# Sums of squares placed half a block later, and the norm of a gated mixing applied behind its matmul

## The reference

```python
def rms_norm(x, g):
    y = x * rsqrt(mean(x * x, axis=-1) + 1e-6)
    return y * g

def swiglu_ffn(h, w_in, w_out):
    gate, up = split(h @ w_in, 2)
    return (silu(gate) * up) @ w_out

def gmlp_chunk_mix(h, w_uv, v_norm, w_s, b_s, w_o):
    u, v = split(gelu(h @ w_uv), 2)          # 2048 features each
    v = rms_norm(v, v_norm)
    sv = einsum('gts,bcsgd->bctgd', tril(w_s), v) + b_s   # mixes the tokens of a chunk of 128
    return (u * sv) @ w_o

for i in range(2):
    x = x + 0.5 * swiglu_ffn(rms_norm(x, ...), ...)
    h = rms_norm(x, mix_norm[i])
    x = x + (rwkv7_time_mix(h) if i == 0 else gmlp_chunk_mix(h))
    x = x + cross_attention(rms_norm(x, ...), memory)
    x = x + 0.5 * swiglu_ffn(rms_norm(x, ...), ...)
```

## Time and profile before

| what | value |
|---|---|
| median of 3 runs | 2070.46 us (2066.52 to 2074.31) |
| the profiled execution | 2068.08 us |
| its span | 2065.9 us |
| granted TensorE clock, mean | 0.98 |
| TensorE busy | 1936.4 us, 94% |
| VectorE busy | 1332.2 us, 64% |
| ScalarE busy | 1054.7 us, 51% |
| weights moved | 288 transfers of 1024 KB |

### The profile page before, as it was taken

One profiled execution on the slowest core, in us unless ns is written; L12 is line 12 of the kernel. 1 busy time (PEld: TensorE's weight loads), 2 busy tenths in 40 slices (PEclk: granted clock), 3 DMA queues, 4 the chain that ended last, 5 costly groups with the idle time before them and its releaser, 6 DMA issues.

```text
span 2065.9 us, 43633 instructions
## 1 busy us (share of the span) xinstructions
PE 1936.4 (94%) x18364; PEld 1892.0 (92%) x18364; DVE 1332.2 (64%) x1652; ACT 1054.7 (51%) x1373; POOL 57.8 (3%) x44
## 2 busy tenths in 40 slices
PE   5999998999998999998988999999999798999998
PEld 5998997899998999997887999999999797999998
DVE  6586579677776755798444665557555646556555
ACT  6555565855556444576523554445444455545443
POOL 0020000000000000000060000000000000000000
PEclk9999999999999999999999999999999899999999
DMA  5743332254553555443400435444455352434553
GB/s 197 227 157 137 135 131 103 102 184 165 185 187 134 183 181 182 145 164 123 144 4 6 161 116 182 181 181 174 175 181 181 133 182 105 166 122 176 181 183 110
DMA packets 51881, 313.35 MB, mean 152 GB/s; under 512 B 13489, under 2 KB 13617, under 8 KB 14257
## 3 DMA queue, kind: packets, MB, share of 16 engines
q1 hardware_dynamic: 51328, 308.42, 42.0%
q10 hardware_dynamic: 432, 3.15, 0.4%
HBM read 310.50 MB, written 1.05 MB: 151 GB/s over the span
## 4 chain that ended last, share of the span: by engine, by line
PE 70%; DVE 18%; ACT 6%; issue 4%; DMA 1%; DVEq 0%; ACTq 0%; SPq 0%
PE ps L282 62%; DVE wl L1892 5%; ACT wh L1267 2%; PE ps L766 2%; DVE pages L2334 1%; DVE work L1921 1%; DMA raw<-in_stream 1%; DVE pages L2149 1%; DVE pages L2396 1%; DVE pages L2151 1%; DVE pages_r L1909 1%; PE ps L941 1%; DVE pages L1965 1%; PE ps L752 1%; DVE h_r L1950 1%
## 5 line engine op out<-in xcount | busy, mean ns | idle before, releaser
L1892 DVE TENSOR_TENSOR wl<-raw,wh 128x1024 fp32r<-128x1024 f32 x576 | 701.3, 1233 | 532.5 <-ACT wh L1267 530.7
L1267 ACT ACTIVATE wh<-raw 128x1024 fp32r<-128x1024 f32 x576 | 597.6, 1052 | 456.2 <-PE ps L282 402.2
L282 PE MATMUL ps<-sq_r,wh 128*128 128x256 f32 x2592 | 742.7, 287 | 15.9 <-DVE h_r L1909 8.3
L282 PE MATMUL ps<-sq_r,wl 128*128 128x256 f32 x2592 | 735.7, 284 | 0.0
L282 PE MATMUL ps<-h_r,wh 128*128 128x256 f32 x2560 | 726.8, 284 | 0.0
L282 PE MATMUL ps<-pages_r,wh 128*128 128x256 f32 x2480 | 548.5, 287 | 33.8 <-DVE pages_r L1909 14.2
L282 PEld LDWEIGHTS ps<-sq_r,wh 128*128 128x128 f32 x2592 | 500.1, 193 | 20.8 <-issue 16.7
L282 PEld LDWEIGHTS ps<-sq_r,wl 128*128 128x128 f32 x2592 | 500.0, 193 | 0.0
L282 PEld LDWEIGHTS ps<-h_r,wh 128*128 128x128 f32 x2560 | 494.1, 193 | 0.5
L282 PE MATMUL ps<-pages_r,wl 128*128 128x256 f32 x1680 | 479.4, 285 | 0.0
L282 PEld LDWEIGHTS ps<-pages_r,wh 128*128 128x128 f32 x2480 | 425.9, 195 | 38.1 <-issue 26.8
(11 more groups left out here) (309 smaller groups left out, 1813.6 us busy)
## 6 DMA issues: line engine op xcount, KB each, us to landing
raw<-in_stream SPq DMA_DIRECT2D x288, 1024.0 KB, 4.8
pages<-in_rpb SPq DMA_DIRECT2D x32, 64.0 KB, 6.5
pages<-in_mem SPq DMA_DIRECT2D x1, 1024.0 KB, 4.9
x<-in_x SPq DMA_DIRECT2D x1, 1024.0 KB, 12.6
pages<-in_mem ACTq DMA_DIRECT2D x1, 1024.0 KB, 4.9
pages<-in_gmlp_b ACTq DMA_DIRECT2D x1, 1024.0 KB, 4.7
pages<-in_gmlp_w ACTq DMA_DIRECT2D x1, 1024.0 KB, 6.8
out<-h SPq DMA_DIRECT2D x4, 256.0 KB, 2.4
```

What stands on the lines that cost most here:

```text
L282: mm = pe.matmul(out, left, right, start=start and q == 0, stop=stop and q == 2, skip_group_check=True)
L1267: f(t.wh[(2 * b0 + hf) % PIECE_SLOTS][:], t.raw[b0 % 2][:, hf * 1024:(hf + 1) * 1024], ACT.Copy).then_inc(s["high_done"], 1)
L1892: tt(t.wl[i][:], t.raw[b0 % 2][:, hf * 1024:(hf + 1) * 1024], t.wh[i][:].bitcast(F32), ALU.subtract).then_inc(s["low_done"], 1)
```

## The change

It has three parts.

1. At `ffn0` to `ffn4`, TensorE's sums of squares move from between the first and the second weight block to the middle of the second one, behind its first half (the new `between` of `up_block`). ScalarE's `high(b + 1)` moves ahead of the first gate step.
2. At `x0` and `x1` the sum moves behind the whole second block, and `high`/`low` of block 1 move ahead of `norm_root` and of the wait for `norm_std`.
3. `mix2` becomes a late norm. `gm_u` is read out by VectorE, scaled by `rstd` (`gate_half`), and ScalarE applies GELU in place. For `gm_v`, whose product is token-major, TensorE makes the sum of squares also as one number per partition (four matmuls with one column into bank 5), ScalarE takes Ln and Exp of it into `stat`, and uses it as the scale of the GELU, which takes two activations of 256 columns instead of one of 512. The two loops over `gm_u` become straight code.

```diff
-LATE = ("ffn0", "ffn1", "x0", "ffn2", "ffn3", "x1", "ffn4")
+LATE = ("ffn0", "ffn1", "x0", "ffn2", "ffn3", "mix2", "x1", "ffn4")
...
-    def up_block(n, bank, b, act, name=None):
+    def up_block(n, bank, b, act, name=None, between=lambda: None):
         for hf in range(2):
+            if hf:
+                between()
             up_piece(n, bank, b, hf, act, name)
...
         up_block(n, n % BANKS, b, norm_parts, name)
-        if f == 1:
-            norm_sum("mem2")
-        norm_sum(name)
-        if f == 1:
-            first_norm_sum(name)
-        up_block(n + 1, (n + 1) % BANKS, b + 1, norm_parts)
+
+        def sums():
+            if f == 1:
+                norm_sum("mem2")
+            norm_sum(name)
+            if f == 1:
+                first_norm_sum(name)
+
+        up_block(n + 1, (n + 1) % BANKS, b + 1, norm_parts, between=sums)
...
         project(f"xq{i}", norm_parts, n=1, name=name)
+        project(f"xq{i}", norm_parts, first=1, n=1)
         norm_sum(name)
-        project(f"xq{i}", norm_parts, first=1, n=2)
+        project(f"xq{i}", norm_parts, first=2, n=1)
...
+    project("gm_u", norm_parts, n=2, name="mix2")
+    pe.wait_ge(s["norm_part"], 2 * NORM["mix2"] + 2)
+    for hf in range(2):
+        for b in range(TB):
+            at_ = hf * T + b * P
+            pe.matmul(ps[:, 5, b:b + 1], norm_partial(t, "mix2")[:, at_:at_ + P], cst(t, "ones")[:, 0:1],
+                      start=hf == 0 and b == 0, stop=hf == 1, skip_group_check=True)
     norm_sum("mix2")
-    operand("mix2")
-    project("gm_u", norm_parts, groups=2)
+    project("gm_u", norm_parts, first=2, n=2)
+    project("gm_u", norm_parts, first=4)
     project("gm_v", norm_parts, groups=2, token=True)
...
+        high(b + 1)
         early(0, 0, 0, True)
-        high(b + 1)
         late(0, 0, 0, True)
...
         late_norm(f"x{i}", prev)
-        highs(f"xq{i}", n=1)
+        highs(f"xq{i}", n=2)
         norm_root(f"x{i}")
-        highs(f"xq{i}", 1, 2)
+        highs(f"xq{i}", 2, 1)
...
-    norm("mix2", last_down(3))
-    take_groups("gm_u", 0, 0, 2, ACT.Gelu_apprx_tanh)
-    v2 = t.pages[:, 2 * FP:4 * FP].rearrange("p (b c) -> p b c", b=TB)
+    late_norm("mix2", last_down(3))
+    highs("gm_u", n=2)
+    act.wait_ge(s["norm_sum"], NORM["mix2"] + 1)
+    f(t.stat[:, 44:46], ps[:, 5, 0:TB], ACT.Ln, scale=1.0 / D, bias=t.stat[:, COL_EPS:COL_EPS + 1]).then_inc(s["gm_root"], 1)
+    norm_root("mix2")
+    act.wait_ge(s["gm_root"], 1)
+    f(t.stat[:, 44:46], t.stat[:, 44:46], ACT.Exp, scale=-0.5).then_inc(s["gm_root"], 1)
+    for k in range(1, 9):
+        if 1 < k < 8:
+            high(BLK["gm_u"] + k)
+        c = slice((k - 1) * 512, k * 512)
+        act.wait_ge(s["u_evac"], SEG["gm_u"] + k)
+        f(t.pages[:, c], t.pages[:, c], ACT.Gelu_apprx_tanh).then_inc(s["gm_up"], 1)
+    act.wait_ge(s["gm_root"], 2)
     for k in range(8):
         high(BLK["gm_v"] + k)
         n, c = SEG["gm_v"] + k, slice(k * 256, (k + 1) * 256)
-        take(n, n % BANKS, BLK["gm_v"] + k, v2[:, :, c], ACT.Gelu_apprx_tanh)
+        act.wait_ge(s["piece_done"], 2 * (BLK["gm_v"] + k) + 2)
+        for b in range(TB):
+            ins = f(t.page[2 + b][:, c], ps[:, n % BANKS, b * 256:(b + 1) * 256], ACT.Gelu_apprx_tanh,
+                    scale=t.stat[:, 44 + b:45 + b])
+        ins.then_inc(s["u_evac"], 1)
...
-        lows(f"xq{i}", n=1)
+        lows(f"xq{i}", n=2)
...
-            if k:
+            if k > 1:
                 low(BLK[f"xq{i}"] + k)
...
-    swiglu(3, "ffn3", last_down(2))
-
-
-    norm("mix2", last_down(3))
+    swiglu(3, "ffn3", last_down(2), "mix2")
+    late_norm("mix2", last_down(3))
+    lows("gm_u", n=2)
+    dve.wait_ge(s["norm_std"], NORM["mix2"] + 1)
+
+    def gate_half(k):
+
+        dve.wait_ge(s["piece_done"], 2 * (BLK["gm_u"] + k) + 2)
+        scaled(t.pages[:, k * 512:(k + 1) * 512],
+               ps[:, (SEG["gm_u"] + k) % BANKS, :].rearrange("p (n t) -> p n t", n=2), 2).then_inc(s["u_evac"], 1)
+
+    gate_half(0)
+    gate_half(1)
+    lows("gm_u", 2, 1)
     dve.wait_ge(s["rows_in"], 32)
...
-    low_groups("gm_u", 0, 2)
+    for k in range(2, 8):
+        gate_half(k)
+        if k < 7:
+            lows("gm_u", k + 1, 1)
     low_groups("gm_v", 0, 2)
+    dve.wait_ge(s["gm_up"], 8)
     dve.wait_ge(s["gm_vnorm"], 8)
```

More of the change, by code:

```diff
@@ L126 @@
 rw_ds0 rw_ds1 rw_s0 rw_s1 rw_turn rw_yt rw_sq rw_var rw_varsb
-rw_std rw_out fin_gain fin_log fin_inv fin_log2 fin_logs fin_std gm_vnorm gm_vstd gm_vout0 gm_vout1 gm_mask gm_mix gm_mixed
+rw_std rw_out fin_gain fin_log fin_inv fin_log2 fin_logs fin_std gm_vnorm gm_vstd gm_vout0 gm_vout1 gm_mask gm_mix gm_mixed gm_root gm_up
 """.split()
```

## The result

The changed kernel takes 2044.15 us (median of 4 runs, 2041.44 to 2047.07), the kernel before 2069.26 us in the same comparison (2066.52 to 2074.31). The ratio is 0.9873, with a 95% interval of 0.9851 to 0.9895: the change makes the kernel 1.3% faster. The prediction was 2048.5 us with a range of 2042 to 2057.

The account below looks back on a forecast made before the run. The kernel was taken as a chain of matmuls on TensorE, busy 94%. 12.7 + 9.6 - 0.3 = 22.0 us off the profiled 2068.1 gave 2046.1; with 2.4 us for the median, 2048.5 us, range 2042 to 2057.

Parts of the forecast that it names:

- The stop at `mix2`: Before `gm_u`, TensorE's 14.11 us stop and 1.77 us of slow matmuls go; net 12.7 us won after added costs.
- the 0.3 of the tail: At the last `gm_v` block, two activations instead of one delay the token mixing: 0.3 us lost.
- the lower bound: Eight one-column passes at `mix2`: at least 0.12 us each, 0.96 us together; 1.0 us taken, 1.7 us from above.
- The moved sums: At ffn0 to ffn4, x0 and x1, TensorE's waits before the sums of squares vanish: 9.6 us won.
- the same 0.1 for each on top: At each of seven moved sums, 0.1 us is added to the 8.9 us of named waits, giving 9.6 us.
- four passes need 0.86: At `ffn3`, the sum's four passes take 0.86 us of the 2.65 us seen, so 1.79 us is saved.
- The slack in the feed-forwards: ScalarE's SiLU slips 2 us behind `high(b + 1)`; an estimated 5 us remain before the first down projection, least at `ffn1`.
- The slack at the attentions: At x0 and x1 the scaled query is ready 5.3 us after block 1, wanted at 6.6 us: 1.3 us slack.
- The slack at `ffn1`: Before the first down projection of `ffn1`, TensorE arrives 0.9 us sooner and some 0.8 us of slack remains.
- The drain: Rival: each table switch drains about 1.4 us more, making the queries at x0 and x1 late; 2051.4 us, chance 0.04.
- The gated mixing: Rival: ScalarE and VectorE, handing one bank back and forth, pace its eight blocks and take back 12.7 us; 2061, chance 0.04.
- The clock: Rival: it drops at the `mix2` sums and stays low through `gm_u` and `gm_v`, losing 75 us; 2124, chance 0.03.

Follow-up runs that it names:

- Experiment 1: The kernel before with only the sums at ffn0 to ffn4, x0 and x1 moved, `mix2` left plain: 2057.22 us, ratio 0.9946.
- experiment 4: The changed kernel with ScalarE's first gate step again ahead of `high(b + 1)` in each feed-forward: 2050.1 us, ratio 0.991.
- experiment 6: The changed kernel with the four one-column matmuls done twice (16 passes instead of 8), same result: 2045.31 us, ratio 0.989.
- experiment 7: The changed kernel with an unused one-column square root added ahead of the root at x0 and x1, to force a table load: 2045.01 us, ratio 0.9893.
- experiment 2: The changed kernel with the seven other sums and the high/low order as before, only `mix2` late: 2053.9 us, ratio 0.9932.
- experiment 3: The changed kernel with x0 and x1 as before on all three engines: 2046.13 us, ratio 0.9896.
- experiment 5: The changed kernel with ScalarE and VectorE in their old order at x0 and x1, TensorE's sum still late: 2045.26 us, ratio 0.9886.

## Why the prediction was right

**The stop at `mix2`: right.** 12.6 us were won on the stretch, 12.4 (12.7 less the 0.3 of the tail) were forecast. The start behind the down projection stops for 0.46 and 0.64 us, as the `ffn3` boundary said (0.47 and 0.65), and the clock stays at 1.00 (2.4 GHz), so the 1.77 us of slow matmuls are won too. The eight one-column passes take 0.81 us, and eight more cost 0.89, where I took 1.0 and called 0.96 the lower bound. The bound was wrong: a pass with one column goes a little below the 0.12 us of an ordinary matmul, at 0.11. The sum costs 0.76 + 0.19 us, forecast 1.04. The `gm_v` tail costs 0.3 us: the pair of activations takes 0.82 us (0.85 in the estimate), and the wait of the token mixing rises from 5.0 to 5.3 us.

**The moved sums: right, undersized by 0.9 us.** The true term is 10.5 us, not 9.6. The step at fault is "the same 0.1 for each on top", and behind it "four passes need 0.86". That price was read in the earlier trace rows up to the start of a fifth pass. The passes start 0.215 us apart there and at `ffn3` alike, but the matmul that follows the last of them starts 0.03 us behind it, so that four passes and the way to the next matmul take 0.68 us. At `ffn3` 2.65 - 0.68 = 1.97 us are won instead of 1.79. Seven times that difference is 1.3 us; less the 0.28 us lost at `x1` that is the 0.9 to within 0.1. Experiment 1 shows that these sums pay by themselves.

**The slack in the feed-forwards: wrong at `ffn0`.** "`ffn1` is smallest" and "the four others have microseconds" do not hold. At `ffn0` there was no slack: TensorE already waited 0.78 us for low halves, because VectorE has a reduction of 3.97 us just ahead of them (from 485.21 in the changed kernel), and with the moved sum it waits 1.14 us. The old order of ScalarE would have made it 2.41 (experiment 4).

**The slack at the attentions: the step that failed.** The estimate of 1.3 us had "ScalarE must first do its high halves", one Copy of 1.06 us from the end of block 1. In fact there are two Copies, and they do not start with the end of the block but with the arrival of the weights. With a transfer of 4.8 to 4.9 us, as at `x0` in the changed kernel and at `x1` in experiments 1 and 6, 1.0 to 1.2 us of slack is left, which is near the estimate by luck. With the 6.2 us at `x1` in the changed kernel none is left: 0.28 us is lost. The price was small, so the total did not suffer. A transfer later by another microsecond would, by this chain, have cost a microsecond. I had costed the reordering on two engines and forgotten the third queue.

**The slack at `ffn1`: it held.** No wait of a down projection on the gate shows. In the changed kernel the first low half for the first down projection is ready at 678.6 and TensorE starts that projection at 679.56, so 0.9 us is left where 0.8 was estimated:

```profile
677.37 2.36 DVE L1920 TENSOR_TENSOR wl<-raw,wh 128x1024 fp32r<-128x1024 f32 x2 [0.26 <-ACT wh L1280]
```

With the old order of ScalarE a wait of 0.88 us appears there (experiment 4), so at this place the reordering is needed.

**The drain: not seen.** The Trainium skill (ScalarE: Activation LUTs, What ACT_TABLE_LOAD costs) puts every switch at about 2.66 us. Here a switch that was added cost 1.50 us including its own 0.2 us function (experiment 7), and the function follows the end of its load within 0.02 us, here and at 40 of the 48 loads of the changed kernel; at the other eight the function waits for its input. The measurement decides. The forecast went by the row of the trace before, and that was the right choice.

**The other rivals.** The gated mixing was not paced by ScalarE or VectorE: no wait of `gm_u` on a bank shows, and the stretch came out at the forecast. The clock did not fall at the sums. The forecast, set against the profiled execution's own time, was 2068.1 - 22.0 = 2046.1 us; the profiled execution of the changed kernel took 2044.25 us. Of the 1.8 us between them 1.1 are the two terms above (0.9 and 0.2), 0.4 the balance of everything else, and 0.3 lies around the spans, whose own difference is 23.5 us. The median of the changed kernel lies another 2.4 us below the forecast because the three runs of before had a median 2.4 us over the profiled one, and those of after do not.

## What to carry to other kernels

When a matrix engine is nearly always busy, a reduction that it waits for need not be faster, only later: move its place by as much work as the reduction is late, and check in the trace what was standing behind it on the other engines. If an instruction is put ahead of a short chain, ask for every one of its inputs, the weight transfer too, when it arrives; an engine that has time is not the same as data that are there. And the price of a group of instructions should be read up to the start of the instruction that will follow it, since what follows may start sooner or later than one more of the same group.

## What the runs showed of the hardware

**The clock is not the same from run to run in the same code.** The stretch from the sum of `mix1` to the first score of `x0` holds the RWKV mixing, with many short waits. Corrected for the moved sum of `x0` (1.5 us) and the added switch, it took from 324.7 to 328.0 us in the profiles of the eleven kernels, which don't differ there. A window of the kernel before and the matching one of the changed kernel show the same work under different granted clocks (the last column but two):

```profile
855.00:882.00 27.00, 23.82 (x176) 23.54 (x175) 23.23 (x39) 15.20 (x20) 0.00 (x0) 0.88 0.46 160
```
```profile
853.00:880.00 27.00, 23.82 (x183) 23.54 (x182) 23.24 (x39) 15.27 (x21) 0.00 (x0) 0.94 0.44 161
```

The same happens behind the token mixing. In the kernel before, `gm_o` started at full clock; in the changed kernel it started at 0.57, and `gm_o` took 47.51 us from its first matmul to its last instead of 46.02:

```profile
1748.00:1752.00 4.00, 4.00 (x36) 4.00 (x35) 3.77 (x7) 1.06 (x1) 0.00 (x0) 1.00 0.02 4
```
```profile
1725.00:1729.00 4.00, 4.00 (x22) 4.00 (x23) 3.97 (x7) 0.00 (x0) 0.00 (x0) 0.57 0.00 0
```

It is no effect of the change: experiment 1, whose gated mixing is that of before, lost 2.5 us there, experiments 2 to 5 and 7, with that of the changed kernel, lost 1.3, 1.3, 2.7, 1.5 and 1.5, and experiment 6, with the same code, lost nothing (46.03 us). What decides it from run to run was not found. For a reader it means that two profiles of this kernel can differ by 3 to 5 us with no edit behind it, and that an edit of 1 us is to be read from its own stretch.

**The length of one weight transfer varies by over a microsecond.** In the eight kernels that sum late at `x1` the transfer for the high halves of query block 1 is issued 5.6 us ahead of the sum, and it took 4.8 us (experiment 1) to 6.2 us (the changed kernel) from issue to landing. What decides it was not found. Behind the start of a late norm ScalarE therefore idles 3.70 us (`x0`), 3.68 us (`mix2`) and 5.10 us (`x1`) for weights in the changed kernel, and only at `x1` does anything come late, by 0.28 us. In the earlier trace rows nothing of it shows, because the root stood ahead.
